# Attention values from split operands, and a reordered begin of the second mixer, in a two-layer hybrid decoder on one core

## The reference

```python
kv = mem_n @ w_kv
k = kv[..., :D_MODEL].reshape(B, M, XA_HEADS, XA_DH).astype(F32)
v = kv[..., D_MODEL:].reshape(B, M, XA_HEADS, XA_DH).astype(F32)
s = jnp.einsum('bthd,bmhd->bhtm', q, k) * (XA_DH ** -0.5)
p = jax.nn.softmax(s, axis=-1)
o = jnp.einsum('bhtm,bmhd->bthd', p, v).reshape(B, T, D_MODEL).astype(h.dtype)
```

## Time and profile before

| what | value |
|---|---|
| median of 3 runs | 3149.55 us (3148.19 to 3152.57) |
| profiled execution | 3150.07 us, its span 3148.3 us |
| mean granted clock of TensorE | 0.993 of full |
| TensorE matmuls busy | 3083.2 us, 98% |
| TensorE weight loads busy | 2514.2 us, 80% |
| VectorE busy | 1907.4 us, 61% |
| ScalarE busy | 1187.0 us, 38% |
| cross-attention of layer 0, products 0 to 7 | 528 to 657 us |
| begin of the second mixer | 1398 to 1448 us |
| cross-attention of layer 1, products 0 to 7 | 2259 to 2388 us |

### The profile page before, as it was taken

One profiled execution on the slowest core, in us unless ns is written; L12 is line 12 of the kernel. 1 busy time (PEld: TensorE's weight loads), 2 busy tenths in 40 slices (PEclk: granted clock), 3 DMA queues, 4 the chain that ended last, 5 costly groups with the idle time before them and its releaser, 6 DMA issues.

```text
span 3148.3 us, 46167 instructions
## 1 busy us (share of the span) xinstructions
PE 3083.2 (98%) x17454; PEld 2514.2 (80%) x17454; DVE 1907.4 (61%) x3049; ACT 1187.0 (38%) x2282; POOL 165.3 (5%) x270
## 2 busy tenths in 40 slices
PE   8999999999999999999999999999999999999997
PEld 6778897777888888877888788889777788888886
DVE  7276646437566666667555566644643756666666
ACT  3335544235332332244111366644423533233222
POOL 0019300000000000000000012100000000000000
PEclk9999999999999999999999899999999999999998
DMA  3110331012111111212222221123101211111122
GB/s 132 34 47 21 120 109 40 27 34 101 47 54 53 53 53 47 94 54 81 98 96 97 80 75 55 56 68 110 38 27 34 100 48 54 53 53 53 47 94 80
DMA packets 81320, 205.99 MB, mean 65 GB/s; under 512 B 6304, under 2 KB 39344, under 8 KB 80176
## 3 DMA queue, kind: packets, MB, share of 16 engines
q1 hardware_dynamic: 40320, 141.91, 14.1%
q10 hardware_dynamic: 40880, 62.41, 5.5%
HBM read 174.93 MB, written 29.36 MB: 65 GB/s over the span
## 4 chain that ended last, share of the span: by engine, by line
PE 86%; DVE 8%; ACT 3%; issue 2%; DMA 1%; ACTq 0%; DVEq 0%; SPq 0%
PE ps L2522 41%; PE ps L2538 14%; PE ps L2779 5%; PE ps L2777 5%; PE ps L2778 5%; PE ps L2943 2%; PE ps L2678 2%; PE ps L2873 1%; DVE work L1476 1%; PE ps L2658 1%; DVE work L1492 1%; DVE hres L1507 1%; DMA wraw<-wstream_dram 1%; PE ps L3075 1%; PE ps L2833 1%
## 5 line engine op out<-in xcount | busy, mean ns | idle before, releaser
L2522 PE MATMUL ps<-act,whi 128*128 128x512 f32 x3664 | 1152.0, 396 | 6.8 <-DVE work L1751 2.5
L2522 PEld LDWEIGHTS ps<-act,whi 128*128 128x128 f32 x3664 | 685.9, 188 | 168.8 <-issue 15.3
L2522 PE MATMUL ps<-act,wlo 128*128 128x512 f32 x1832 | 717.3, 392 | 0.0
L1460 DVE TENSOR_TENSOR wlo<-wraw,whi 128x1024 fp32r<-128x1024 f32 x257 | 313.9, 1222 | 306.3 <-ACT whi L692 303.4
L692 ACT ACTIVATE whi<-wraw 128x1024 fp32r<-128x1024 f32 x214 | 225.5, 1056 | 581.2 <-DMA wraw<-wstream_dram 578.3
L2522 PEld LDWEIGHTS ps<-act,wlo 128*128 128x128 f32 x1832 | 344.2, 188 | 75.8
L2538 PE MATMUL ps<-act,whi 128*128 128x512 f32 x1376 | 370.9, 391 | 0.7 <-DVE work L2037 0.7
L2538 PEld LDWEIGHTS ps<-act,whi 128*128 128x128 f32 x1376 | 258.8, 188 | 57.1 <-issue 1.9
L1882 DVE TENSOR_TENSOR work<-work,ps 128x512 f32<-128x512 f32 x336 | 225.1, 685 | 103.8 <-PE ps L2779 103.8
L2538 PE MATMUL ps<-act,wlo 128*128 128x512 f32 x688 | 213.0, 391 | 0.0
L2522 PE MATMUL ps<-hid,whi 128*128 128x512 f32 x512 | 160.0, 394 | 1.2 <-DVE hidf L1734 0.9
(11 more groups left out here) (335 smaller groups left out, 4840.1 us busy)
## 6 DMA issues: line engine op xcount, KB each, us to landing
wraw<-wstream_dram SPq DMA_DIRECT2D x262, 512.0 KB, 3.6
qkvz<-work ACTq DMA_DIRECT2D x32, 512.0 KB, 2.7
work<-qkvz ACTq DMA_DIRECT2D x64, 256.0 KB, 3.3
hsave<-hres ACTq DMA_DIRECT2D x2, 4096.0 KB, 12.1
hres<-hsave ACTq DMA_DIRECT2D x2, 4096.0 KB, 12.7
hres<-xT_dram ACTq DMA_DIRECT2D x8, 512.0 KB, 11.5
hres<-xT_dram ACTq DMA_DIRECT2D x1, 4096.0 KB, 13.6
outT_dram<-hres SPq DMA_DIRECT2D x16, 256.0 KB, 2.0
```

Of the source, the lines that this page charges most:

```text
L1460: TT(wlo[s][:], wraw[s][:], whi[s][:].bitcast(F32), ALU.subtract).then_inc(w_split, 1)
L2522: last = mm(out_of(u)[:, 0:width], (wlo if hl else whi)[s][:, at:at + P], rhs(kt, xp, e), start=kt == hl == xp == 0, stop=kt == kts - 1 an ...
```

## The change

Values and probabilities are split as the projections' operands are. ScalarE writes the transposed probabilities to `pth` as fp32r (in the place of unit 15), and VectorE's new `probability_lo(i)` subtracts that from the same two PSUM banks into half of `spare`. ScalarE's new `value_hi` and VectorE's `value_lo` split the values of heads 0 and 1 ahead of product 0, and those of heads 2 and 3 ahead of product 4; the low part lies where the values were. `weighted` has twelve fp32r matmuls in place of four float32 ones. In the output projection `two(6)` stands after step 0 of the fourth unit, and no longer ahead of it. At the layer's end `boundary` gets `ahead`: with `ahead=KT` all eight squares stand ahead of rstd of POST_B. VectorE evacuates unit 14 at t = 4, right behind unit 13, and no longer at t = 5.

```diff
+        vsplit = place("vsplit", WORK + 12 * UNIT, [P, 2, SEQ], F32R)
+        pth = place("pth", WORK + 15 * UNIT, [P, 2, HALF], F32R)
+        spare = place("spare", WORK + 6 * UNIT, [P, 2, SEQ], F32R)
...
+        def values_of(i):
+            first, hl = (spare[:, :, E[0]], vsplit[:, :, E[0]]) if i < 4 else (vsplit[:, :, E[0]], vsplit[:, :, E[1]])
+            return first, hl
...
-            def boundary(b, gain, k0, u_next, before_hi, after_hi):
+            def boundary(b, gain, k0, u_next, before_hi, after_hi, ahead=4):
...
-                for t in range(2, 4):
+                for t in range(2, ahead):
                     pre_square(b, t, 0)
                 rstd(b, POST_B)
-                for t in range(4, KT):
+                for t in range(ahead, KT):
                     pre_square(b, t, 0)
...
+                def value_hi(i):
+                    if i:
+                        eng.wait_ge(xa_v, k8 + 4)
+                    else:
+                        eng.wait_ge(v_ready, 4 * (layer + 1))
+                        eng.wait_ge(h_new, 16 * b + 8)
+                    A(values_of(i)[0], work[:, 12:14, E[i // 4]], ACT.Copy).then_inc(xa_vhi, 1)
...
-                    A(pt, bank(6, 2), ACT.Copy).then_inc(xa_pt, 1)
+                    A(pth[:], ps[:, 6:8, :], ACT.Copy).then_inc(xa_pt, 1)
...
                 rest_squares(b)
+                value_hi(0)
                 transposed(0)
...
                     probabilities(i)
+                    if i == 4:
+                        value_hi(4)
                     transposed(i)
...
+                def value_lo(i):
+                    eng.wait_ge(xa_vhi, 2 * layer + i // 4 + 1)
+                    vh, vl = values_of(i)
+                    TT(vl, work[:, 12:14, E[i // 4]], vh.bitcast(F32), ALU.subtract).then_inc(xa_vlo, 1)
+
+                def probability_lo(i):
+                    eng.wait_ge(xa_pt, k8 + i + 1)
+                    TT(spare[:, :, E[1]], ps[:, 6:8, :], pth[:].bitcast(F32), ALU.subtract).then_inc(xa_plo, 1)
...
                 normalise(0)
+                value_lo(0)
+                probability_lo(0)
                 normalised(norm_no(b, PRE_B))
...
                 query(7)
+                probability_lo(1)
...
                     normalise(i)
+                    if i == 4:
+                        value_lo(4)
+                    probability_lo(i)
...
                 splits(ux)
+                probability_lo(5)
                 output(5)
...
                 result_lo(3)
+                probability_lo(6)
...
                 result_lo(6)
+                probability_lo(7)
...
-                        total(u, 9 + t)
+                        if t != 5:
+                            total(u, 9 + t)
+                        if t == 4:
+                            total(u, 14)
...
                 def weighted(i):
                     h = HEADS[i][0]
-                    eng.wait_ge(xa_pt, k8 + i + 1)
+                    eng.wait_ge(xa_vlo, 2 * layer + i // 4 + 1)
+                    eng.wait_ge(xa_plo, k8 + i + 1)
+                    vh, vl = values_of(i)
+                    ph, pl = pth, spare[:, :, E[1]]
                     for d in range(XA_T):
+                        at = (h % 2) * N_MEM + d * P
                         for m in range(2):
-                            at = h * N_MEM + d * P
-                            last = mm(bank(6 + d), v[:, m, at:at + P], pt[:, m * HALF:(m + 1) * HALF], start=m == 0,
-                                      stop=m == 1)
+                            mm(bank(6 + d), vh[:, m, at:at + P], ph[:, m, :], start=m == 0, stop=False)
+                            mm(bank(6 + d), vh[:, m, at:at + P], pl[:, m, :], start=False, stop=False)
+                            last = mm(bank(6 + d), vl[:, m, at:at + P], ph[:, m, :], start=False, stop=m == 1)
...
-                two(6)
-                units([(n + 3, ux + 3)], 0)
+                units([(n + 3, ux + 3)], 0, after={0: lambda: two(6)})
...
-                    boundary(b, "mix_pre_g", KT, plan.at["mix1"][1], total, lambda: None)
+                    boundary(b, "mix_pre_g", KT, plan.at["mix1"][1], total, lambda: None, ahead=KT)
```

More of the change, by code:

```diff
@@ L402, in build @@
             sem(f"xa_{k}") for k in ("scores", "transposed", "weighted", "max", "exp", "norm", "pt", "out"))
+        xa_vhi, xa_vlo, xa_plo = sem("xa_v_hi"), sem("xa_v_lo"), sem("xa_pt_lo")
         hid_hi, hid_ready = sem("hid_hi"), sem("hid_ready")
@@ L837, in attention @@
                 mx, den = small[:, 256:260], small[:, 264:268]
-                p, pt = unit(14), unit(15)
+                p = unit(14)
+                def value_hi(i):
[5 more added lines that the diff above has]
+                    A(values_of(i)[0], work[:, 12:14, E[i // 4]], ACT.Copy).then_inc(xa_vhi, 1)
                 def probabilities(i):
@@ L2643, in attention @@
                 kk = unit(8, 2).rearrange("p (t m) -> p t m", m=N_MEM)
-                v = work[:, 12:14, :]
-                p, pt = unit(14), unit(15)
+                p = unit(14)
                 def scores(i):
```

## The result

The changed kernel takes 3128.51 us in the median of 4 executions (3127.58 to 3130.32) against 3148.87 us beside it: a ratio of 0.9935, 95% interval 0.9923 to 0.9947. That is 20.4 us less. The forecast was 16.1 us less, 3133.5 us, with a range from 3130 us.

A forecast was written before the change was run, and what follows sets the result against it. TensorE's stream was taken as the bound, 3083.2 us busy in a span of 3148.3 us. Products 11.0 us plus the second mixer's begin 5.1 us gave 16.1 us less, 3133.5 us; own range 3131 to 3136, with rivals 3130 to 3141 us.

The forecast's parts named there:

- The product: At `weighted`, 12 fp32r matmuls at 228 ns take 2.74 us, 0.69 us less; 16 products give 11.0 us.
- The operands: Ahead of each product, VectorE's 20 new subtractions and ScalarE's 4 copies are hidden; margin 0.4 us at products 6 and 7.
- Rival A: Low halves late at products 6 and 7 (perhaps 0): 4 places x 0.8 to 1.2 us, 3137 to 3138 us; 10 %.
- The begin of the mixer: Second mixer: TensorE's two stops go, VectorE's second-half chain starts 5.1 us earlier, so the end moves by 5.1 us.
- Rival B: Second mixer's begin gives only its first part, 2.5 us, as squares or VectorE's chain are held: 3136 us; 12 %.
- The rest: At the second mixer's begin, TensorE's gain beyond 5.1 us turns into waits for low parts (L1497), 1 to 1.7 us.
- The sum: Whole kernel: 11.0 + 5.1 = 16.1 us off the profiled 3150.07 us gives 3134.0 us, median near 3133.5 us.
- the fall at 1420: Second mixer's begin: slow clock behind TensorE's second stop, granted 0.70 of full in 1420 to 1425, counted in TensorE's own gain.
- Rivals C and D: At the 16 products: C, spacing slower than the projections', 3172 us, 2 %; D, well under 228 ns, 3112 us, 1 %.

The follow-up runs named there:

- lo_twice: Changed kernel with each probability subtraction done twice, one behind the other; one execution, read for waits, not time: TensorE waits four times, only ahead of products 6 and 7.
- delay10: Changed kernel with 44 extra matmuls (10.0 us) ahead of the last unit before the delta-rule loop: mean 3140.5 us against 3128.8 us.
- before_delay10: Kernel before with 44 extra matmuls (10.0 us) ahead of the last unit before the delta-rule loop: mean 3158.5 us against 3149.2 us.
- fill_begin: Kernel before with 7 extra matmuls (4.5 us) in its two idle gaps at the second mixer's begin, nothing reordered: mean 3147.9 us against 3149.2 us.
- stop_again: Changed kernel with TensorE made to wait at the mixer's begin, ahead of its fourth unit, for the second new residual tile: mean 3130.7 us against 3128.8 us.

## Why the prediction was wrong

**The product** (12 matmuls at 228 ns, 0.69 us less, 16 times): right. 2.74 us in the chain, 5.44 and 5.45 us for the two layers, 10.9 for 11.0. The Trainium skill's figure of about 131 ns in a stream ("TensorE: Matmul & The Clock Gate", "Back-to-back issue gap") didn't come: the distance is 228 ns.

**The operands** (hidden, margin 0.4 us at products 6 and 7): right, shown by the absence of waits and by what doubling and moving did. Rival A did not come. Its condition is real: lo_twice brings it about, and TensorE then waits 3.9 us.

**The begin of the mixer** (5.1 us, the chain on VectorE behind rstd decides): right. The chain starts 9.99 us earlier than before, where TensorE had come 4.64 us earlier into this stretch: 5.35 us. Rival B did not come. The rest did turn into waits for low parts, 1.4 us in all at this place (1 to 1.7 us were forecast). The fall of the clock there is gone.

**The sum** is where it failed. The step is the one that takes 11.0 + 5.1 = 16.1 us from the profiled execution's 3150.07 us and comes to "the median should be near 3133.5 us", with a range that held only the matmuls' spacing, the mixer's begin and "scatter of a median, about 1 us". It took all that lies outside the edits as constant: the change in clock loss away from them was put at nothing, without a reason, while the trace of before had 10.3 us of lost clock at the loop's entry. I had read only the fall at 1420. What the runs showed in its place: 20.3 us between the means of the two kernels, of which about 16 are work by three comparisons. With the gaps at the entry filled in both kernels the difference is 16.6 us, with the mixer's stops of the kernel before filled as well 15.2 us, and between the executions of both kernels at clock 0.996, five and eleven of them, 16.8 us. The other 4 us or so are clock that the changed kernel loses less of: 0.9962 against 0.9941, or 6.6 us of full clock in a span. About 1.7 us of that is the fall at 1420, which went with the stop.

**Rivals C and D** did not come: no spacing over or under that of the projections.

**Still open** is why the loop's entry, 350 us behind the last edit, loses less clock in the kernels with the mixer's reorder. Neither the place in time alone (delay10, before_delay10) nor the stop itself (fill_begin, stop_again) shows as the cause. Kernels with both edits had 0.9952 to 0.9962, without them 0.9938 to 0.9941, with one or with the stops filled 0.9945 to 0.9949. The clock follows the number of stops left at the mixer's begin, but there is one trace to a kernel (two of the changed one), too few to say how often the loop's early fall comes with each. That the gaps there are needed for the loss is shown, what decides whether and when they bring it is not.

## What to carry to other kernels

Before a forecast of a few microseconds, list every stretch in which the granted clock is under 1.00, also those that the change doesn't touch, and put their loss into the range: here it was 10 us of full clock, up to 6.8 us of time, in a stretch 350 us away, and it varied from one execution to the next. To tell work from clock, compare executions at equal clock, or fill the idle gaps in both kernels with matmuls that nobody reads. Where operands are split just ahead of a product, the cover is counted in matmuls between the transposes and the product: 12 of them (2.75 us) hid a copy and a subtraction of 128x1024 with 0.3 us to spare, 9 of them left a wait of 0.4 us.

## What was unexpected in the hardware

The same passage of the loop, with the same instructions, took between 500.2 and 505.6 us from mark to mark, and 498.9 to 499.5 us where ten matmuls in the idle gaps kept the clock at 1.00; what the traces show to differ is the clock. In the kernel before, TensorE idle for 2 of 4 us ahead of 1780 was followed by the lower level for much of 30 us. In the changed kernel the same 2 of 4 us ahead of 1770 were followed by 14 us at full clock, and it fell to the lower level only at 1784, behind another 2 us in which TensorE was busy for 0.8 us. At the kernel's end two sums over partitions took 2.08 us in one execution and 1.14 us in the other.
